# A two-block transformer on one core: another order of the conv mixer's tail

## The chip, the cores and the metric

One core of a Trainium2 chip (trn2) runs the whole program in one launch. The metric is the device time of one execution in microseconds (us); less is better. TensorE (PE) does the matrix products, VectorE (DVE), ScalarE (ACT) and GpSimd (POOL) the elementwise work, and SyncE (SP) only issues the loads.

## The reference

Two transformer blocks, one after the other, on 256 tokens of width 2048. The change lies in the first block's mixer, a gated causal convolution of width 31 per channel with a LayerNorm:

```python
mod = silu(c) @ mod_w + mod_b                # 6 vectors: shift, scale, gate, for each half of the block
h = rms_norm(x, norm1_g) * (1 + sc1) + sh1
a, gt = split(h @ conv_w_in + conv_b_in)     # 2048 -> 2 x 2048
u = a * sigmoid(gt)
u = depthwise_conv(u, conv_dw_w, 31 taps) + conv_dw_b
u = silu(layer_norm(u, conv_ln_g, conv_ln_b))
x = x + (1 + g1) * (u @ conv_w_out + conv_b_out)
# then h2 = rms_norm(x) modulated by sh2, sc2, an MLP, and a second block (attention and FFN)
```

All data are fp32. `mod_w` alone is 2048 x 12288, and it is read in 192 pieces of 128 x 1024.

## The kernel before

**Engines.** The program is written by one thread of Python that calls `A.put`, `V.put`, `T.put`, `P.put` (ACT, DVE, PE, POOL) and `Y.load` (SP). Each engine executes its own calls strictly in the order in which they were put; waits between engines are semaphores given as `after`. So where a call stands in the order of the Python code decides what stands behind it on its engine.

**Stream.** All weights come as 512 KB items through a ring of stage slots: 12 slots in the conv-in phase, 6 (`NSTAGE`) after it. The list `seq` fixes the order of items. An item is a product tile (256 rows of weights by 512 columns) or one of 16 tiles of a modulation chunk. `consume()` takes the next item and then starts what loads fit. `mix(main, extra)` spreads the extras evenly between the main items.

**Modulation.** The chunks for `0,2` (the gate) and `0,1,*` (shift and scale of the second norm) are done "aside": ACT multiplies a tile by the column of silu(c) into one of three product buffers (`R<-stage,CS`), and POOL adds it to the sum (`R<-R`); the first tile of a chunk goes straight into the sum without an add. There are 80 such tiles: `N_MOD_IN` of them are mixed into the last 46 tiles of conv-in, `N_MOD_TAIL` into the tail, and the rest into the conv-out tiles up to `N_MOD_OUT`. The last chunk (`0,1,3`, 16 tiles) is done by PE (`bank<-stage,CS`) in the tail between conv-in and conv-out.

**Conv-in.** 8 chunks p = 0..7 of 8 tiles each; chunk p gives channel tiles 2p and 2p+1 (`ct`). The first three are interleaved. `products()` calls `pe_tile(g)` and then `between_tiles()` for each tile. At the end of a chunk the task `first` copies the banks out on ACT (`scr<-bank`, "evacuation"). `gated` comes one tile later (`later(1, gated)`): 8 transposes on PE, the sigmoid on ACT, and two DVE operations that write u (`R2f<-bank,PA,scr`).

**Taps.** As soon as the u of a job in `DVE_JOBS` are there, `dve_job` puts its steps into `dve_taps`: a step is two DVE operations of 128x256 (`bank<-R2f,DW,bank`), one for each of two chains. Jobs of two channel tiles have 31 steps, the single ones, (13,) and (15,), 16 steps; then comes `end`, which copies the result out on ACT (`R2f<-bank`). ct 3 and 14 (`PE_JOBS`) are done by PE as 31 products with diagonal matrices (`bank<-R2f,hx`), in pieces of 8 taps from `pe_taps`.

**LayerNorm.** When the taps of ct 0 to 12 are over, `ln_provisional` runs one tile later: 13 PE products (26 records in the trace) sum them, DVE makes a provisional mean m0, and `slow` gets seven `centre` tasks (DVE subtracts m0 from two channel tiles), each followed by a square on ACT and its sum on PE. `ln_late(ct)` does the same for 13, 14, 15 (DVE subtraction, PE sum, ACT square, PE sum) and is called at once when the taps of such a ct end. `layer_norm()` turns the sums into mean and variance on DVE and ACT, and its `finish` tasks apply scale, Silu and the split into the two parts `hhi`, `hlo` for conv-out. Conv-out tiles are split too: ACT makes `whi`, DVE `wlo`, and PE needs three products for each fp32 product.

**What is called between two tiles** (`between_tiles`), in this order: up to two tasks, up to two delayed tasks that are due, one or more of `slow`, up to `TAPS_A_TILE` = 5 steps of `dve_taps`, one piece of `pe_taps`.

**After the last conv-in tile** the tail's two loops run (lines from `while tasks or delayed` to `layer_norm()` below). Their order of calls is what the change rewrites.

Of the kernel before, what the change touches and what calls it, by code (L numbers as in the profile page):

```python
# [11 lines left out]
ACT = mybir.ActivationFunctionType  # L12
# [4 lines left out]
NKT = D // 128  # L17
TAPS = 31
# [8 lines left out]
L_LHS = 1  # L27
L_PROJ = 6
N_MOD_IN = 66
N_MOD_TAIL = 4  # L30
N_MOD_OUT = 14
TAPS_A_TILE = 5
L_PE_JOB = 2
L_SQUARE = 2
L_SUMS = 3
# [2 lines left out]
PE_JOBS = (3, 14)  # L38
LN_LATE = (13, 14, 15)
# [69 lines left out]
def build_program(nc, a, out):  # L109
    ctx = ExitStack()  # L110
    with ctx:
        def sb(name, shape, dt=F32):
            return ctx.enter_context(nc.sbuf_tensor(name, shape, dt))

        def sem(name):
            return ctx.enter_context(nc.semaphore(name))
# [25 lines left out]
        ST = sb("ST", [128, 64])  # L142
# [12 lines left out]
        A = Engine(nc.scalar, sem("s_act"))  # L155
# [4 lines left out]
        def line(name):  # L160
# [20 lines left out]
        consts = P.put(nc.gpsimd.affine_select, out=ident[:, :], in_=ident[:, :], compare_op=ALU.not_equal,  # L181
                       fill=1.0, base=0, pattern=[[-1, 128]], channel_multiplier=1, after=[t])
        eps = ST[:, 60:61]
# [52 lines left out]
        buf, _, loaded = raw["Z"]  # L236
# [7 lines left out]
        tasks, slow = deque(), deque()  # L244
        dve_taps, pe_taps = deque(), deque()
# [4 lines left out]

        delayed, tile_no = [], [0]

        def later(n, task):

            delayed.append((tile_no[0] + n, task))
# [7 lines left out]
        def between_tiles():  # L263
            tile_no[0] += 1
            for _ in range(min(2, len(tasks))):
                tasks.popleft()()
            due = [d for d in delayed if d[0] <= tile_no[0]][:2]
            for d in due:
                delayed.remove(d)
            for d in due:  # L270
                d[1]()
            for _ in range(min(len(slow), 1 + len(slow) // 10)):
                slow.popleft()()
            for _ in range(min(len(dve_taps), TAPS_A_TILE)):
                dve_taps.popleft()()
            if pe_taps:
                pe_taps.popleft()()
# [16 lines left out]
        pair_ready = []  # L294
# [445 lines left out]
        ln = {}  # L740
# [53 lines left out]
        def diag_of(ct, j):  # L794
            return diag_store[ct][:, j // 2, 128 * (j % 2):128 * (j % 2) + 128]
# [6 lines left out]
        def pe_job(ct):  # L802

            job = {}

            def part(lo, hi_):
                if lo == 0:
                    job["bank"] = misc.take()
                b, bank, free = job["bank"]
                for j in range(lo, hi_):  # L810
                    t = T.put(nc.tensor.matmul, bank[:, 0:S], diag_of(ct, j), U[:, ct, j:j + S], start=(j == 0),
                              stop=(j == TAPS - 1), after=[diags[ct, j], u_ready[ct]] + free)
                if hi_ == TAPS:
                    conv_done[ct] = A.put(nc.scalar.activation, CV[:, ct, :], bank[:, 0:S], ACT.Identity,
                                          bias=PA[:, 48 + ct:49 + ct], after=[t, params["A"]])
                    misc.give(b, conv_done[ct])
                    conv_finished(ct)
            for lo in range(0, TAPS, 8):
                pe_taps.append(lambda lo=lo: part(lo, min(lo + 8, TAPS)))

        waiting_jobs = deque(DVE_JOBS)

# [7 lines left out]
        def conv_finished(ct):  # L830
            taps_over.add(ct)
            early = [k for k in range(NKT) if k not in LN_LATE]
            if ct in early and all(k in taps_over for k in early):
                later(1, lambda: ln_provisional(early))
            if ct in LN_LATE and "m0" in ln:
                ln_late(ct)
# [8 lines left out]
        def conv_in_epilogue(p):  # L845
            def start(pair, done, free_group):
                def first():
                    got = evacuate(pair, done)
                    free_group(got[0][2], got[1][2])

                    def gated():
                        two = [misc.take(), misc.take()]
                        for gate in (1, 0):
                            _, bank, free = two[gate]
                            for k in range(2):
                                for tok in range(2):
                                    kk = 2 * gate + k
                                    _, buf, made = got[tok]
                                    t = T.put(nc.tensor.transpose,
                                              bank[:, k * 256 + tok * 128:k * 256 + tok * 128 + 128],  # L860
                                              buf[:, kk * 128:(kk + 1) * 128], ident[:, :],
                                              after=[made, consts] + free)
                            if gate:
                                gates_in = t
                        for i, _, _ in got:
                            tiles.give(i, t)
                        i, sig, free = tiles.take()
                        for k in range(2):
                            ct = 2 * p + k
                            r = A.put(nc.scalar.activation, sig[:, k * S:(k + 1) * S], two[1][1][:, k * S:(k + 1) * S],  # L870
                                      ACT.Sigmoid, bias=PA[:, 32 + ct:33 + ct], after=[gates_in, params["A"]] + free)
                        for k in range(2):
                            ct = 2 * p + k
                            u_ready[ct] = V.put(nc.vector.scalar_tensor_tensor, out=U[:, ct, PAD:PAD + S],
                                                in0=two[0][1][:, k * S:(k + 1) * S], scalar=PA[:, 16 + ct:17 + ct],
                                                in1=sig[:, k * S:(k + 1) * S], op0=ALU.add, op1=ALU.mult,
                                                after=[t, r, params["A"], consts])
                        misc.give(two[1][0], r)
                        misc.give(two[0][0], u_ready[ct])
                        tiles.give(i, u_ready[ct])  # L880
                        jobs_ready()
                        for ct in (2 * p, 2 * p + 1):
                            if ct == PE_JOBS[1]:
                                pe_job(ct)
                            elif ct in PE_JOBS:
                                later(L_PE_JOB, lambda ct=ct: pe_job(ct))
                    later(1, gated)
                tasks.append(first)
            return start

# [60 lines left out]
        def layer_norm():  # L951
# [3 lines left out]
                          after=[ln["total"]])  # L955
            t = V.put(nc.vector.tensor_tensor, va[:, 0:S], mu[:, S:2 * S], mu[:, S:2 * S], ALU.mult,
                      after=[shift] + free)
# [2 lines left out]
            misc.give(ln["sums"][0], shift)  # L960
            misc.give(ln["squares"][0], t)
            t = A.put(nc.scalar.activation, va[:, S:2 * S], va[:, 0:S], ACT.Sqrt, bias=eps, scale=1.0, after=[t])
            shifts = mu[:, None, S:2 * S].to_broadcast([128, 2, S])
            factors = va[:, None, 0:S].to_broadcast([128, 2, S])
            pairs = range(0, NKT, 2)
# [101 lines left out]
        for q in range(4):  # L1067
            co += chunk(a["conv_w_out"][0], q * 512, 0, NKT, (hhi, hlo), s_ready,
                        residual_epilogue(q, 0, 2))
        tail = mix(mod_pairs(0, 1, 3, aside="PE", soon=True), mods[N_MOD_IN:N_MOD_IN + N_MOD_TAIL])  # L1070
        seq += tail + co[:3] + mix(co[3:N_MOD_OUT], mods[N_MOD_IN + N_MOD_TAIL:]) + co[N_MOD_OUT:]
        n_tail = n_first[0] + len(tail)
# [414 lines left out]
        products_of.freed[2] = list(params.values()) + [cond]  # L1487
        products(0, n1)
        conv_in_read[0] = pe_done[-1]
        while tasks or delayed:  # L1490
            run_one()
            for _ in range(min(len(dve_taps), 4)):
                dve_taps.popleft()()
        while dve_taps or pe_taps or slow or tasks or delayed or len(ln["late"]) < len(LN_LATE):
            for _ in range(2):
                if tasks or delayed:
                    run_one()
            if pe_taps:
                pe_taps.popleft()()
            for _ in range(min(len(dve_taps), 4)):  # L1500
                dve_taps.popleft()()
            if slow:
                slow.popleft()()
            if consumed[0] < n_tail:
                consume()
        while consumed[0] < n_tail:
            consume()
        while len(pair_ready) < 2:
            consume()
        A.put(nc.scalar.activation, ST[:, 61:62], eps, ACT.Sqrt, after=[consts])  # L1510
        layer_norm()
        ln["taps_done"] = conv_done[NKT - 1]
        products(n1, n2)
        norm_phase(1, h2_ready, pe_done[-1])
# [19 lines left out]
                       after=[pe_done[-1]])  # L1534
# [68 lines left out]
```

How the kernel before makes its waits and increments, by code:

```python
    def run(self):  # L82
        for fn, args, kw, sem, k in self.queue:
            made = fn(*args, **kw)
            if sem is not None:
                made.then_inc(sem, k)
```

## Time and profile before

| | before |
|---|---|
| median of three runs | 2721.91 us (2720.96 to 2722.74) |
| the profiled execution | 2721.52 us, span 2719.7 us |
| TensorE busy | 2549.7 us, 94% of the span |
| VectorE, ScalarE, GpSimd busy | 1693.2, 1146.8 and 618.9 us |
| mean granted clock of TensorE | 0.975 of full speed |
| last conv-in product ends, first conv-out product starts | about 331 and 423.9 us |

The profiled execution took 1.8 us more than its span and lies 0.4 us below the median. PE's busy time is modelled (a product that waits in the pipeline counts as busy), so the stages are read by starts and by what each engine waited for. Times in the rows are us from the span's start.

### The profile page before, as it was taken

To read this page: it belongs to the slowest core of one execution; us is meant where nothing else is said; L and a number is where in the kernel's file an instruction comes from. 1 tells how busy PE (TensorE), PEld (TensorE's weight loads), DVE (VectorE), ACT (ScalarE), POOL (GpSimd) and SP (SyncE) were. 2 spreads that over 40 slices of the span, in tenths; PEclk is the share of its full clock that TensorE was granted. 3 is DMA by queue.
4 is the path that set the end of the run, shared out by engine and by line. 5 is a ranking of instruction groups with operands and counts; after the bars stand their busy time and mean duration, and the time that the engine had idled before them with its cause. 6 is when DMAs were issued, how large, how long until landed. Compare 5 with 4: busy or idle time off the path is not lost. (4 is left out here: it accounts for less than half of the span.)

```text
span 2719.7 us, 29378 instructions
## 1 busy us (share of the span) xinstructions
PE 2549.7 (94%) x10784; PEld 1979.6 (73%) x10784; DVE 1693.2 (62%) x2024; ACT 1146.8 (42%) x1441; POOL 618.9 (23%) x277
## 2 busy tenths in 40 slices
PE   4899987899999999999889999989899999999998
PEld 2354445678888888887677788767688888888886
DVE  6678847667877767768563242396476655555455
ACT  2144416444343443444444454533444434443443
POOL 1058814012222222222223334434200000000000
PEclk9999988999999999999889999999899999999999
DMA  9989746668888988988644546797578766666664
GB/s 319 375 287 365 240 152 207 198 221 288 305 300 284 314 295 289 311 293 302 151 129 134 178 141 193 226 316 242 182 245 280 249 192 188 192 186 192 194 188 140
DMA packets 340158, 644.66 MB, mean 237 GB/s; under 512 B 30000, under 2 KB 63440, under 8 KB 338992
## 3 DMA queue, kind: packets, MB, share of 16 engines
q1 hardware_dynamic: 338752, 642.09, 71.9%
q8 instruction: 87, 1.43, 0.2%
q0 software_dynamic: 448, 0.43, 0.1%
q14 instruction: 55, 0.45, 0.0%
q10 hardware_dynamic: 816, 0.26, 0.0%
HBM read 640.60 MB, written 2.10 MB: 236 GB/s over the span
## 5 line engine op out<-in xcount | busy, mean ns | idle before, releaser
L84 ACT ACTIVATE whi<-stage 128x1024 fp32r<-128x1024 f32 x752 | 795.6, 1059 | 1034.2 <-PE bank L84 891.2
L84 DVE TENSOR_TENSOR wlo<-stage,whi 128x1024 fp32r<-128x1024 f32 x588 | 749.1, 1275 | 751.7 <-ACT whi L84 726.5
L84 PE MATMUL bank<-whi,hhi 128*128 128x512 f32 x2016 | 808.2, 401 | 41.7 <-DVE hlo L84 18.9
L84 PE MATMUL bank<-whi,hlo 128*128 128x512 f32 x2016 | 792.2, 393 | 0.0
L84 PE MATMUL bank<-wlo,hhi 128*128 128x512 f32 x2016 | 791.8, 393 | 0.0
L84 POOL TENSOR_TENSOR wlo<-stage,whi 128x1024 fp32r<-128x1024 f32 x164 | 411.3, 2508 | 1058.4 <-ACT whi L84 995.0
L84 PEld LDWEIGHTS bank<-whi,hhi 128*128 128x128 f32 x2016 | 383.5, 190 | 133.2 <-ACT scr L84 23.6
L84 PEld LDWEIGHTS bank<-wlo,hhi 128*128 128x128 f32 x2016 | 383.7, 190 | 80.6 <-issue 3.1
L84 PEld LDWEIGHTS bank<-whi,hlo 128*128 128x128 f32 x2016 | 382.7, 190 | 81.8
L84 PE MATMUL bank<-whi,uhi 128*128 128x512 f32 x992 | 390.0, 393 | 0.0
L84 PE MATMUL bank<-whi,ulo 128*128 128x512 f32 x992 | 389.3, 392 | 0.0
L84 PE MATMUL bank<-wlo,uhi 128*128 128x512 f32 x992 | 387.4, 391 | 0.0
L84 DVE SCALAR_TENSOR_TENSOR acc<-stage,CS,acc 128x1024 f32<-128x1024 f32 x165 | 235.5, 1427 | 18.0 <-DMA stage<-in_mod_w 14.6
L84 POOL TENSOR_TENSOR R<-R 128x1024 f32<-128x1024 f32 x75 | 183.2, 2445 | 270.4 <-ACT R L84 262.6
L84 PE MATMUL bank<-stage,hx 128*128 128x512 f32 x512 | 232.7, 613 | 10.8 <-DMA stage<-in_conv_w_in 6.6
L84 PEld LDWEIGHTS bank<-wlo,uhi 128*128 128x128 f32 x992 | 186.3, 188 | 41.4 <-issue 0.2
L84 PEld LDWEIGHTS bank<-whi,ulo 128*128 128x128 f32 x992 | 186.3, 188 | 40.8
L84 PEld LDWEIGHTS bank<-whi,uhi 128*128 128x128 f32 x992 | 186.4, 188 | 40.3 <-issue 1.1
L84 PEld LDWEIGHTS bank<-stage,hx 128*128 128x128 f32 x512 | 99.3, 197 | 134.4 <-issue 121.2
L84 DVE SCALAR_TENSOR_TENSOR bank<-R2f,DW,bank 128x256 f32<-128x256 f32 x418 | 165.4, 483 | 0.0
L84 DVE SCALAR_TENSOR_TENSOR R<-stage,CS,R 128x1024 f32<-128x1024 f32 x105 | 134.3, 1279 | 11.4 <-DMA stage<-in_mod_w 9.0
L84 PE MATMUL bank<-ident,scr 128*128 128x128 f32 x524 | 83.2, 302 | 47.0 <-DVE scr L84 41.8
(120 smaller groups left out, 1219.8 us busy)
## 6 DMA issues: line engine op xcount, KB each, us to landing
stage<-in_mlp_w SPq DMA_DIRECT2D x256, 512.0 KB, 5.4
stage<-in_mod_w SPq DMA_DIRECT2D x192, 512.0 KB, 7.1
stage<-in_w_ada SPq DMA_DIRECT2D x192, 512.0 KB, 5.4
stage<-in_w_in SPq DMA_DIRECT2D x136, 512.0 KB, 3.9
stage<-in_w_ffn_gate SPq DMA_DIRECT2D x88, 512.0 KB, 4.4
stage<-in_w_ffn_up SPq DMA_DIRECT2D x88, 512.0 KB, 4.5
stage<-in_w_ffn_down SPq DMA_DIRECT2D x88, 512.0 KB, 4.2
stage<-in_conv_w_in SPq DMA_DIRECT2D x128, 256.0 KB, 7.3
```

The source lines that it names most:

```text
L84: made = fn(*args, **kw)
```

## The change

Five edits of order, none of the arithmetic.

1. **Pace of the taps.** Instead of 5 steps a tile, `between_tiles` keeps an estimate: every tile adds 4.1 us, every step 0.8 us, and steps are put until they are 5.0 us ahead of the tiles. With no taps waiting the taps' clock is set to the tiles'.
2. **Gated units of the last chunk** (p = 7) run at once after its evacuation instead of among the delayed tasks.
3. **PE's taps** of ct 14 are one piece of 31 instead of four pieces of 8; those of ct 3 stay as they were.
4. **The tail's loop.** The first loop runs only `tasks`, and without DVE steps. In the second, PE's taps come first, then up to 3 DVE steps (4 before), then up to two tasks, one of `slow`, one item of the stream. `layer_norm()` is put right after that loop, ahead of the items that are left; before, it came behind them and behind two conv-out items. One more small ACT operation (a Silu on 128x1) is put behind LayerNorm's square root.
5. **Modulation tiles**: 9 instead of 4 in the tail, so 5 instead of 10 among the conv-out tiles (from tile 3 up to 10 instead of up to 14).

```diff
-N_MOD_TAIL = 4
-N_MOD_OUT = 14
-TAPS_A_TILE = 5
+N_MOD_TAIL = 9
+N_MOD_OUT = 10
+LEAD = 5.0
+TILE_US = 4.1
+STEP_US = 0.8
...
-            for _ in range(min(len(dve_taps), TAPS_A_TILE)):
+            pace["tile"] += TILE_US
+            if not dve_taps:
+                pace["taps"] = max(pace["taps"], pace["tile"])
+            while dve_taps and pace["taps"] < pace["tile"] + LEAD:
+                pace["taps"] += STEP_US
                 dve_taps.popleft()()
...
-            for lo in range(0, TAPS, 8):
-                pe_taps.append(lambda lo=lo: part(lo, min(lo + 8, TAPS)))
+            for lo in range(0, TAPS, 8 if ct == PE_JOBS[0] else TAPS):
+                pe_taps.append(lambda lo=lo: part(lo, min(lo + (8 if ct == PE_JOBS[0] else TAPS), TAPS)))
...
-                    later(1, gated)
+                    if p == NKT // 2 - 1:
+                        tasks.append(gated)
+                    else:
+                        later(1, gated)
...
             t = A.put(nc.scalar.activation, va[:, S:2 * S], va[:, 0:S], ACT.Sqrt, bias=eps, scale=1.0, after=[t])
+            A.put(nc.scalar.activation, ST[:, 62:63], eps, ACT.Silu, after=[consts])
...
-        while tasks or delayed:
+        while tasks:
             run_one()
-            for _ in range(min(len(dve_taps), 4)):
+        while dve_taps or pe_taps or slow or tasks or delayed or len(ln["late"]) < len(LN_LATE):
+            if pe_taps:
+                pe_taps.popleft()()
+            for _ in range(min(len(dve_taps), 3)):
                 dve_taps.popleft()()
-        while dve_taps or pe_taps or slow or tasks or delayed or len(ln["late"]) < len(LN_LATE):
             for _ in range(2):
                 if tasks or delayed:
                     run_one()
-            if pe_taps:
-                pe_taps.popleft()()
-            for _ in range(min(len(dve_taps), 4)):
-                dve_taps.popleft()()
             if slow:
                 slow.popleft()()
             if consumed[0] < n_tail:
                 consume()
+        A.put(nc.scalar.activation, ST[:, 61:62], eps, ACT.Sqrt, after=[consts])
+        layer_norm()
         while consumed[0] < n_tail:
             consume()
-        while len(pair_ready) < 2:
-            consume()
-        A.put(nc.scalar.activation, ST[:, 61:62], eps, ACT.Sqrt, after=[consts])
-        layer_norm()
```

## Rows read from the trace of the kernel before

**Rows 1.** By stage: start:end, length; busy us of PE, PEld, DVE, ACT, POOL; clock, DMA share, GB/s.

```profile
150.00:331.00 181.00, 176.83 (x493) 88.15 (x492) 154.53 (x389) 82.50 (x100) 144.28 (x67) 0.99 0.87 306
331.00:424.00 93.00, 66.54 (x215) 35.07 (x213) 47.57 (x99) 30.03 (x43) 24.01 (x11) 0.85 0.48 161
424.00:536.00 112.00, 99.33 (x416) 79.05 (x416) 79.84 (x78) 61.85 (x82) 29.78 (x10) 0.94 0.63 195
```

**Rows 2.** What ACT waited for, 210 to 331 us: us in total, times, longest.

```profile
ACT R L84 <- POOL R L84: 33.7, 23, 8.8
ACT R2f L84 <- DVE bank L84: 29.7, 4, 11.3
```

**Rows 3.** DVE in order of time, conv-in: start, us, operation, count [idle before it].

```profile
213.35 2.43 DVE L84 SCALAR_TENSOR_TENSOR bank<-R2f,DW,bank 128x256 f32<-128x256 f32 x6
216.51 0.99 DVE L84 TENSOR_SCALAR bank<-R2f,DW,PA 128x256 f32<-128x256 f32 x2 [0.73 <-ACT R2f L84]
...
243.56 0.88 DVE L84 SCALAR_TENSOR_TENSOR R2f<-bank,PA,scr 128x256 f32<-128x256 f32 x2 [2.56 <-PE bank L84]
...
256.21 1.29 DVE L84 SCALAR_TENSOR_TENSOR G<-bank,G 128x512 f32<-128x512 f32 x2
...
275.65 0.88 DVE L84 SCALAR_TENSOR_TENSOR R2f<-bank,PA,scr 128x256 f32<-128x256 f32 x2 [5.61 <-ACT scr L84]
...
307.73 0.88 DVE L84 SCALAR_TENSOR_TENSOR R2f<-bank,PA,scr 128x256 f32<-128x256 f32 x2 [5.61 <-ACT scr L84]
```

**Rows 4.** ACT in order of time around the ends of two tap jobs.

```profile
270.07 0.66 ACT L84 ACTIVATE R2f<-bank 128x256 f32<-128x256 f32 x2 [11.31 <-DVE bank L84]
270.62 1.15 ACT L84 ACTIVATE R<-stage,CS 128x1024 f32<-128x1024 f32 x1
271.66 1.09 ACT L84 ACTIVATE scr<-bank 128x512 f32<-128x512 f32 x2
...
282.55 1.15 ACT L84 ACTIVATE R<-stage,CS 128x1024 f32<-128x1024 f32 x1 [1.35 <-POOL R L84]
...
302.16 0.66 ACT L84 ACTIVATE R2f<-bank 128x256 f32<-128x256 f32 x2 [10.94 <-DVE bank L84]
```

**Rows 5.** PE in order of time, end of conv-in to the first conv-out product.

```profile
306.74 24.20 PE L84 MATMUL bank<-stage,hx 128*128 128x512 f32 x56
...
330.77 5.78 PE L84 MATMUL bank<-R2f,ones 128*128 128x256 f32 x26
344.05 3.58 PE L84 MATMUL bank<-ones,R 128*128 128x1 f32 x16 [7.50 <-POOL R L84]
348.24 1.94 PE L84 MATMUL bank<-ident,scr 128*128 128x128 f32 x8 [0.61 <-DVE MC L84]
...
358.01 5.39 PE L84 MATMUL bank<-R2f,hx 128*128 128x256 f32 x16
...
405.05 7.03 PE L84 MATMUL bank<-stage,CS 128*1 128x512 f32 x16 [1.04 <-DMA stage<-in_mod_w]
423.88 0.77 PE L84 MATMUL bank<-whi,hhi 128*128 128x512 f32 x1 [11.80 <-DVE hlo L84]
```

**Rows 6.** DVE in order of time, tail.

```profile
332.92 0.55 DVE L84 TENSOR_SCALAR bank<-R2f,DW,PA 128x256 f32<-128x256 f32 x1
...
337.05 2.26 DVE L84 TENSOR_TENSOR R2f<-R2f,scr 128x512 f32<-128x512 f32 x1
...
351.14 0.87 DVE L84 SCALAR_TENSOR_TENSOR R2f<-bank,PA,scr 128x256 f32<-128x256 f32 x2
...
361.54 0.69 DVE L84 TENSOR_TENSOR R2f<-R2f,scr 128x512 f32<-128x512 f32 x1
```

**Rows 7.** Groups of instructions, 331 to 424 us: busy us, mean ns | idle before.

```profile
L84 PE MATMUL bank<-stage,CS 128*1 128x512 f32 x64 | 28.4, 592 | 1.0 <-DMA stage<-in_mod_w 1.0
```

**Rows 8.** The same groups, 424 to 484 us, and 484 to 531 us behind the dots.

```profile
L84 DVE TENSOR_TENSOR wlo<-stage,whi 128x1024 fp32r<-128x1024 f32 x14 | 33.8, 2455 | 6.6 <-ACT whi L84 4.3 <-issue 2.3
...
L84 DVE TENSOR_TENSOR wlo<-stage,whi 128x1024 fp32r<-128x1024 f32 x17 | 20.8, 1225 | 19.7 <-ACT whi L84 19.7
```

More of the change, by code:

```diff
@@ L251, in build_program @@
         delayed, tile_no = [], [0]
+        pace = {"tile": 0.0, "taps": 0.0}
         def later(n, task):
```

## The prediction, made before the changed kernel was run

> **What bounds the kernel now.** I read the stages first, then what ACT waited for, then DVE, ACT and PE in order of time. By stage [rows 1], conv-in (150 to 331 us) keeps PE near full in the modelled figures, with the loads at 0.87 of their share. The tail (331 to 424 us) is the weak place: PE busy 66.5 of 93 us, clock 0.85, loads at 0.48. In the conv-out stage PE is busy 99.3 of 112 us. The tail is where the change works, but conv-in is where two of its edits act first, so both have to be followed.
>
> In conv-in the reader should look at ACT. It waited 29.7 us on four occasions for DVE's taps [rows 2]: it stands at the copy-out of a job that DVE has not finished, with an evacuation and modulation copies queued behind it. DVE is then idle 5.61 us before each new u, in two rounds alike [rows 3]. That is a loop: taps end, copy-out, copies, evacuation, transposes, sigmoid, u, next taps. It gives 32.1 us a round (275.65 to 307.73), where 8 tiles cost PE 27.7 (24.20 us for 7 tiles [rows 5], 3.46 each). So conv-in runs by this loop as much as by PE. The copies also wait 33.7 us for POOL [rows 2], and in such a stretch one comes every 2.5 us (1.15 and 1.35 idle [rows 4]).
>
> In the tail the chain is: last conv-in product 330.8, transposes of the last gated unit only at 348.24, behind a 7.50 us wait for POOL's last sum (344.05) [rows 5]; u at 351.14 [rows 6]; taps of 14 and 15 side by side; the modulation products; then 11.80 us of waiting for LayerNorm, conv-out from 423.88 [rows 5].
>
> **The change part by part.** All is counted as a shift of the first conv-out product, for behind it no order changes but the number of aside tiles.
>
> *Pace of the taps.* The estimate has 4.1 us a tile, PE needs 3.46. A round begins with at most one tile between empty taps and new ones, so 12 steps are put in its first tile and 5.1 a tile then; a job of 31 steps and its `end` are over 5 tiles after their start, where 5 a tile took 7. DVE works no faster for it, as it has its steps in either case; only the place of `end` in ACT's order moves, by two tiles. With 66 copies on 46 tiles (1.43 a tile) that puts some three more copies between `end` and the evacuation. The first three cost 1.04 each (three product buffers are free by then), each further one waits for POOL, 2.5 us.
> - Jobs (0,1), (2,4): these sit on a backlog in which nobody waits for the evacuation; 0. The last three steps of (2,4) no longer stand behind u of p = 3: today they run at 213.35 and (5,6) starts at 216.51 [rows 3]. Gain 3.1.
> - u of p = 4: `end` came behind the evacuation, now three copies and the evacuation come behind `end`. Taps over at 237.9, +0.6 copy-out, +3.1 copies, +1.1 evacuation, +2.3 for the next copy, transposes and sigmoid: 245.0 against 243.56. +1.4, the gain of 3.1 used up.
> - u of p = 5: between copy-out and evacuation one copy today (270.07, 270.62, 271.66 [rows 4]), then four, and two more before the sigmoid. Taps end to u goes from 5.6 to 0.6 + 3.1 + 1.4 + 1.1 + 4.9 = 11.1. +5.5.
> - u of p = 6: five copies for two, one of them a first tile of a chunk that needs no POOL, and one before the sigmoid: 9.7 for 5.6, +4.1; but DVE's two gate sums (1.29 [rows 3]) now come behind the taps, -1.3. Together +2.8.
>
> u of p = 6 comes 9.7 us later. From below: 0, if DVE's idle time takes the copies in. From above: all three rounds lose POOL two tiles of work, 3 x 2 x 1.43 x 2.45 = 21.
>
> *The provisional mean.* `end` of (11,12) is put after tile 61, so `ln_provisional` stands on PE ahead of tiles 63 and 64 instead of behind them. It needs the copy-out, 25.9 us after u of p = 6 (307.73 to 332.92 [rows 3, 6], +0.7); PE gets there after 5 tiles, 16.2 us after u. PE waits 9.7 us with two tiles of the last chunk behind it. The 26 records cost 5.8 [rows 5], and after such a wait 3 more: the first ones after idle take 5.39 for 16 (0.337 each), not 0.222 [rows 5]. Then m0, 0.4.
>
> *Gated unit first.* On PE it no longer stands behind the 7.50 us wait. But on DVE all 16 steps of job (13,) are put by tile 64, ahead of it (12.5 at 0.79 a step, 24.4 us for 31 [rows 3, 6]), with m0 and three `centre` in between. A `centre` takes 0.69 alone and 2.26 beside POOL [rows 6]; I take 2.0, POOL having a backlog. So u of p = 7 comes 25.9 + 8.8 + 0.4 + 12.5 + 6.0 = 53.6 us after u of p = 6, against 43.4 today. +10.2. With the full clock and 0.69: 46.7, +3.3. PE and ACT are ready some 8 us before DVE, which hides what they do.
>
> On the second price, the Trainium skill ("SBUF — State Buffer", section "SBUF: two separate sides") has the port pair of DVE and POOL as an exclusive lock for a whole instruction. By it each `centre` could wait for a whole POOL add, 0.69 + 2.35 = 3.0, and this step would be 3 us more; the trace's 2.26 is the one case here and stays below that.
>
> *One piece of taps.* `part` ends with `ln_late(14)`: its DVE subtraction waits for PE's 31 products and stands ahead of all taps of 15. Today they run side by side. From u of p = 7: 1.0 + 14.1 (62 records of 0.227) + 3 slow clock + 0.5 copy = 18.6; late work of 14 and 13's end 2.5; 16 steps 12.5; four `centre` 2.8; mod columns 1.4; end of 15 and its late work 2.5: 40.3. Today about 38.
>
> *LayerNorm first, five more tiles.* Six passes of the loop take only three PE tiles; 14 stand behind the last square. At 0.444 a record, four a tile [rows 7], 24.9 us. The loads are slower: 19 items are outstanding when the slots move again (19 tail and conv-out items; a full share would be 306/0.87 = 352 GB/s, 1.49 us an item [rows 1]; I take 1.42, a little better than that mean, with nothing else on the queue), 27.0 + 1.8 for the first slot + 1.2 landing = 30. LayerNorm itself and its waits lie under that. Left at the end: one `whi`, two Silu, `hhi`, `hlo`, 3.4. So conv-out starts 40.3 + 33.4 = 73.7 after u of p = 7, today 72.7 (351.14 to 423.88). +1.0. The 11.80 us wait [rows 5] shrinks to some 8, and the five tiles (7.1 us of loads) take the rest. From below -6 (loads well ahead), from above +6. The small Silu costs 0.2 and moves a table load under the tiles.
>
> *Conv-out.* Beside POOL's adds `wlo` takes 2455 ns, without them 1225 [rows 8]; 15 tiles last 60 us there, the next 17 only 47. Of the 18.6 us over, slow clock, LayerNorm's finish and the mod columns have some 8; the ten aside tiles about 1.0 each. Five fewer: -5, bounds -2 and -9.
>
> **Sum:** 9.7 + 10.2 + 1.0 - 5.0 = +15.9, on the profiled 2721.5 us: 2737.4; the median lies 0.4 above that run. I say 2737.5.
>
> **Rivals.**
> - *The gated unit wins its 12 us.* The 7.50 us wait and the 4.2 us of mod columns behind it (344.05 to 348.24 [rows 5]) are no longer ahead of it: u 11.7 earlier, -11.7 + 1 - 5 = -15.7, 2706. For it: the 7.50 us wait is real. It decides if less than half of job (13,) stands ahead of that unit on DVE and `end` costs ACT nothing. Against it: 332.92 plus m0, three `centre` and 12.5 is past 347 even if no one waits. Chance 0.10.
> - *Nothing in sum.* The earlier `end` is taken in by idle time (0), the provisional wait costs its lower bound (+3.3), +1, -5: 2721. For it: PE ran 56 records without a gap in the last round, and only POOL and DVE sums are behind the copies. Chance 0.18.
> - *POOL bounds conv-in.* It is busy 144 of 181 us [rows 1]; if every stop of ACT is lost to it, the first term is 21: 2749, and up to 2752 with 3 us of port waits. Chance 0.10.
> - The forecast, 2729 to 2746: 0.60. The rest, 0.02, is beyond.
>
> **Range and chances.** 0.2% is 5.4 us, about what a measurement of this kernel tells from no change. 2714 to 2752 leaves out the first rival and what lies above the third. Slower: the forecast, the third rival and a part of the second, 0.73; within 0.2%: 0.14; faster: 0.13. Most of the chance is on one side; the likeliest case's own range is 2729 to 2746.
>
> **What would show it.** Right: ACT idle before `R2f<-bank` grows from about 11 to 15 us and more in the rounds of p = 5 and 6, and DVE's idle time before u from 5.61 to about 11 and 10; PE idle about 10 us before `bank<-R2f,ones`, with 16 conv-in records behind it; u of p = 7 near 371; DVE idle some 15 us until PE's taps of 14 are over; conv-out near 444. Wrong: u of p = 6 by 309; the sums ahead of all conv-in products on PE without a wait; u of p = 7 before 350; conv-out before 424. Most fragile is the count of copies behind `end`: if stage items are late there, ACT waits for DMA and not for POOL, and the first term changes.

## The result, and the profile after

The changed kernel took 2736.21 us (median of five runs, 2729.96 to 2737.79) against 2721.91 (five runs, 2720.07 to 2723.47): a ratio of 1.0047, 95% interval 1.0032 to 1.0062. It is 14.3 us slower. The profiled execution took 2732.52 us, span 2730.7.

One thing has to be known before the two traces are compared: the programs do not start alike. The first u is written at 153.29 us in the kernel before and at 150.35 in the changed one; over the fourteen traces of this study (one of each kernel) it lies between 150.35 and 155.37, and what follows it in conv-in repeats to 0.1 us wherever the order is the same. So places are given below from the first u. The last conv-out stage ends with the first transposes of the next norm (536.44 before, 545.95 after).

| us from the first u | before | after | shift | forecast shift |
|---|---|---|---|---|
| u of p = 3 | 59.3 | 61.2 | +1.9 | 0 |
| u of p = 6 | 154.4 | 165.8 | +11.3 | +9.7 |
| u of p = 7 | 197.9 | 210.7 | +12.8 | +19.9 |
| first conv-out product | 270.6 | 287.8 | +17.2 | +20.9 |
| first transposes behind conv-out | 383.2 | 395.6 | +12.4 | +15.9 |

The places put the loss at 12.4 us. The medians differ by 14.3, and the spans of the two profiled executions by 11.0: the changed one had its first u 2.9 us earlier and lost 1.5 behind the last place of the table.

The last conv-in round and the loop through ACT, in order of time. First DVE, with the first two u (before, the second came 8.74 us behind the first) and the rounds that answer to [rows 3]. Three dots mark lines left out:

```profile
150.35 0.88 DVE L86 SCALAR_TENSOR_TENSOR R2f<-bank,PA,scr 128x256 f32<-128x256 f32 x2 [13.46 <-PE bank L86]
...
152.03 12.63 DVE L86 SCALAR_TENSOR_TENSOR bank<-R2f,DW,bank 128x256 f32<-128x256 f32 x32
164.56 0.88 DVE L86 SCALAR_TENSOR_TENSOR R2f<-bank,PA,scr 128x256 f32<-128x256 f32 x2
...
243.41 0.88 DVE L86 SCALAR_TENSOR_TENSOR R2f<-bank,PA,scr 128x256 f32<-128x256 f32 x2 [6.64 <-ACT scr L86]
...
281.10 0.88 DVE L86 SCALAR_TENSOR_TENSOR R2f<-bank,PA,scr 128x256 f32<-128x256 f32 x2 [11.21 <-ACT scr L86]
...
306.28 1.28 DVE L86 SCALAR_TENSOR_TENSOR G<-bank,G 128x512 f32<-128x512 f32 x2
316.13 0.88 DVE L86 SCALAR_TENSOR_TENSOR R2f<-bank,PA,scr 128x256 f32<-128x256 f32 x2 [8.56 <-ACT scr L86]
```

The idle times 2.56, 5.61 and 5.61 [rows 3] have become 6.64, 11.21 and 8.56 (with the gate sums, now behind the taps, 9.8 from taps to u). What fills them is on ACT, to be read against [rows 4]: the copy-out waits 15.41 us instead of 11.31, and behind it stand four modulation copies, not one, before the evacuation (`scr<-bank`).

```profile
269.92 0.66 ACT L86 ACTIVATE R2f<-bank 128x256 f32<-128x256 f32 x2 [15.41 <-DVE bank L86]
270.46 3.22 ACT L86 ACTIVATE R<-stage,CS 128x1024 f32<-128x1024 f32 x3
274.13 1.15 ACT L86 ACTIVATE R<-stage,CS 128x1024 f32<-128x1024 f32 x1 [0.45 <-POOL R L86]
275.19 1.06 ACT L86 ACTIVATE scr<-bank 128x512 f32<-128x512 f32 x2
```

Over 210 to 331 us ACT's wait for the taps is 43.0 us, against 29.7 [rows 2] (us in total, times, longest):

```profile
ACT R2f L86 <- DVE bank L86: 43.0, 3, 15.4
ACT R L86 <- POOL R L86: 28.8, 22, 8.8
```

PE from the provisional mean to conv-out, against [rows 5]:

```profile
333.69 4.91 PE L86 MATMUL bank<-R2f,ones 128*128 128x256 f32 x22
341.88 2.08 PE L86 MATMUL bank<-R2f,ones 128*128 128x256 f32 x4 [3.28 <-ACT R2f L86]
343.75 7.65 PE L86 MATMUL bank<-stage,hx 128*128 128x512 f32 x16
...
361.95 15.37 PE L86 MATMUL bank<-R2f,hx 128*128 128x256 f32 x62 [7.34 <-DVE R2f L86]
...
427.83 1.88 PE L86 MATMUL bank<-stage,CS 128*1 128x512 f32 x4 [0.47 <-DMA stage<-in_mod_w]
438.17 0.77 PE L86 MATMUL bank<-whi,hhi 128*128 128x512 f32 x1 [8.46 <-ACT scr L86]
```

The sums do stand ahead of 16 conv-in records, but 22 of their 26 records run without waiting; only the last four, for the channels just copied out, wait, and that for 3.28 us. Behind that wait the granted clock is 0.50 (341.8 to 343.7 us), and the four records take 2.08 us where the 22 took 4.91. And DVE, against [rows 6]: three `centre` of 2.57, 1.37 and 0.68 us, then u of p = 7, then 15.97 us of nothing until PE's taps of 14 are over.

```profile
344.45 2.57 DVE L86 TENSOR_TENSOR R2f<-R2f,scr 128x512 f32<-128x512 f32 x1
...
350.92 1.37 DVE L86 TENSOR_TENSOR R2f<-R2f,scr 128x512 f32<-128x512 f32 x1
...
356.91 0.68 DVE L86 TENSOR_TENSOR R2f<-R2f,scr 128x512 f32<-128x512 f32 x1
...
361.04 0.86 DVE L86 SCALAR_TENSOR_TENSOR R2f<-bank,PA,scr 128x256 f32<-128x256 f32 x2
377.87 0.42 DVE L86 TENSOR_TENSOR R2f<-R2f,scr 128x256 f32<-128x256 f32 x1 [15.97 <-ACT R2f L86]
```

The end of the chain, from the last modulation tile (over at 429.71) to the first conv-out product (438.17), on ACT and then on DVE:

```profile
430.51 1.06 ACT L86 ACTIVATE whi<-stage 128x1024 fp32r<-128x1024 f32 x1 [0.21 <-DMA stage<-in_conv_w_out]
431.87 1.06 ACT L86 ACTIVATE whi<-stage 128x1024 fp32r<-128x1024 f32 x1 [0.30 <-DMA stage<-in_conv_w_out]
433.23 1.06 ACT L86 ACTIVATE whi<-stage 128x1024 fp32r<-128x1024 f32 x1 [0.30 <-DMA stage<-in_conv_w_out]
434.19 1.08 ACT L86 ACTIVATE scr<-R2f,PA 128x256 f32<-128x256 f32 x2
435.30 0.63 ACT L86 ACTIVATE hhi<-scr 128x512 fp32r<-128x512 f32 x1
...
436.01 1.41 DVE L86 TENSOR_TENSOR R2f<-R2f,scr 128x512 f32<-128x512 f32 x2
437.33 0.69 DVE L86 TENSOR_TENSOR hlo<-scr,hhi 128x512 fp32r<-128x512 f32 x1
```

### The profile page after: what moved, and what is told of

Read it like the earlier page. It is cut to its first block and busy times, and to the rows that moved or that the text cites. A ratio compares the mean times of both kernels' runs of the same rounds, so it can differ in the third digit from the quotient of the medians.

```text
span 2730.7 us, 29383 instructions
## 1 busy us (share of the span) xinstructions
PE 2550.4 (93%) x10784; PEld 1976.8 (72%) x10784; DVE 1685.0 (62%) x2024; ACT 1146.9 (42%) x1442; POOL 613.6 (22%) x277
## 5 line engine op out<-in xcount | busy, mean ns | idle before, releaser
L86 DVE TENSOR_TENSOR wlo<-stage,whi 128x1024 fp32r<-128x1024 f32 x588 | 738.6, 1257 | 758.3 <-ACT whi L86 735.3
L86 PEld LDWEIGHTS bank<-whi,hhi 128*128 128x128 f32 x2016 | 384.0, 190 | 125.2 <-ACT scr L86 22.2
L86 POOL TENSOR_TENSOR R<-R 128x1024 f32<-128x1024 f32 x75 | 177.7, 2370 | 270.7 <-ACT R L86 263.3
```

The source lines that it names most:

```text
L86: made = fn(*args, **kw)
```

## The experiments

Twelve kernels, four to a chip. Ratios are to the kernel before on the same chip; its median was 2723.49, 2722.52 and 2722.19 us on the three chips. The steps are compared by their places in us from the first u, in this table; "u6" and "u7" are the u of p = 6 and 7, and "LN" is the DVE operation that forms the variance.

| | ratio (95%) | u6 | u7 | LN | conv-out | behind conv-out |
|---|---|---|---|---|---|---|
| before | 1 | 154.4 | 197.9 | 263.8 | 270.6 | 383.2 |
| after | 1.0047 (1.0032 to 1.0062) | 165.8 | 210.7 | 251.4 | 287.8 | 395.6 |
| e1 old pace | 0.999 (0.9978 to 1.0003) | 154.4 | 189.8 | 238.0 | 274.1 | 382.0 |
| e2 new pace alone | 1.0084 (1.0071 to 1.0097) | 165.8 | 220.1 | 284.8 | 291.6 | 404.1 |
| e3 DVE's taps first | 1.0014 (1.0006 to 1.0023) | 165.8 | 208.3 | 239.6 | 278.0 | 384.0 |
| e4 LayerNorm behind | 1.0057 (1.0044 to 1.0069) | 165.8 | 210.7 | 251.3 | 290.5 | 397.2 |
| e5 tiles as before | 1.004 (1.0025 to 1.0056) | 165.8 | 210.7 | 252.5 | 282.5 | 393.3 |
| e6 gated unit later | 1.0055 (1.004 to 1.007) | 165.8 | 221.8 | 257.2 | 295.0 | 402.6 |
| e8 mean later | 1.0058 (1.0043 to 1.0073) | 165.8 | 205.2 | 254.1 | 291.6 | 399.5 |
| e9 = e1 + e3 | 0.998 (0.9971 to 0.9989) | 154.4 | 189.9 | 231.3 | 268.4 | 375.5 |
| e11 = e3, pace 3.46, lead 0 | 0.9996 (0.9986 to 1.0005) | 151.7 | 183.2 | 242.0 | 273.0 | 381.0 |
| e12 = e9 + items ahead | 0.9944 (0.9929 to 0.9959) | 154.4 | 189.8 | 236.8 | 262.5 | 369.4 |
| e13 = e9 + finish ahead | 0.996 (0.9944 to 0.9975) | 154.4 | 189.8 | 231.4 | 266.7 | 373.1 |
| e14 = e12 + e13 | 0.9945 (0.9928 to 0.9962) | 154.4 | 189.8 | 238.7 | 262.6 | 369.8 |

**e1: the pace undone.**

```diff
-            while dve_taps and pace["taps"] < pace["tile"] + LEAD:
-                pace["taps"] += STEP_US
+            for _ in range(min(len(dve_taps), 5)):
                 dve_taps.popleft()()
```

> The changed kernel with 5 steps a tile again. My theory: the pace puts the copy-out of each tap job two tiles earlier in ACT's order, and costs 8.4 us by the u of p = 6 and keeps all 16 steps of job (13,) ahead of the last gated unit. So u of p = 6 returns to about 307.7, the sums of the provisional mean start without a wait, u of p = 7 comes at about 344, conv-out starts at about 419, and the time is about 2716. Rival (the pace is harmless, the tail's other edits cost the time): u of p = 6 stays near 316 and the time near 2736.

Measured: 2720.44 us, 0.999. u of p = 6 is back at 154.4, to the tenth, and u of p = 7 comes at 189.8, 8.1 before the old place. The rival is out. But conv-out comes at 274.1, not some 5 earlier: the 16 us in which DVE waits for PE's taps now have eight steps of 13 and all 16 of 15 behind them. In the changed kernel the pace thus costs 13.7 us at the first conv-out product. The other four edits together are worth 1.2 us at the end of conv-out, and nothing that the runs can tell from no change.

**e2: the pace alone**, in the kernel before, with the changed kernel's estimate.

> The kernel before with the new pace of the taps and nothing else. My theory: DVE's idle time before u grows from 2.6, 5.6 and 5.6 us to about 6.6, 11 and 8.6 in the three rounds, u of p = 6 comes at about 317, u of p = 7 at about 361, and the time is about 2732. Rival (the pace only costs together with the other edits): within 3 us of the kernel before, 2722.

Measured: 1.0084, 21 us at the end of conv-out. More than I expected. U of p = 6 is 11.4 late, for the 9 expected, and u of p = 7 is 22.2 late, not 10. PE shows why:

```profile
367.33 1.22 PE L86 MATMUL bank<-R2f,ones 128*128 128x256 f32 x2 [7.98 <-DVE R2f L86]
...
373.13 1.97 PE L86 MATMUL bank<-ident,scr 128*128 128x128 f32 x8 [0.52 <-DVE MC L86]
```

The 8 records at 373.13 are the last gated unit. With the new pace job (13,) ends before it in the order, so the late work of 13 stands ahead of it on PE (7.98 us of waiting), and the mod columns too. In the changed kernel the gated unit is put first.

**e6: the last gated unit among the delayed tasks again**, in the changed kernel.

```diff
-                    if p == NKT // 2 - 1:
-                        tasks.append(gated)
-                    else:
-                        later(1, gated)
+                    later(1, gated)
```

> The changed kernel with the last gated unit among the delayed tasks again. My theory: with the new pace the late work of 13 and the mod columns come ahead of it on PE, and u of p = 7 comes some 9 us later, as it did with the pace alone; conv-out some 8 us later; time about 2744. Rival (DVE's 16 steps of 13 stand ahead of that u in either order, so the order on PE is hidden, as my prediction had it): at most 2 us, 2738.

u of p = 7 comes 11.1 us later and conv-out 7.2 later, as the theory says; the rival (hidden by DVE) is out. The timed ratio, 1.0055, is only 0.0008 above that of the changed kernel and the intervals overlap; the place of the steps is shown, the size at the end (2 us by the ratios, 7 by the places) stays open. Beside e2 it says what the edit does under the new pace: it takes back what the pace would otherwise cost there.

**e8: the provisional mean behind all conv-in products.**

```diff
-                later(1, lambda: ln_provisional(early))
+                later(3, lambda: ln_provisional(early))
```

> The changed kernel with the provisional mean put two tiles later, behind all conv-in products, where it stood before. Theory A (what the trace of the changed kernel shows): only the last two of 13 products waited, 3.3 us, and DVE 2.6; so u of p = 7 comes some 3 us earlier and conv-out 1 to 3 us; time about 2733. Theory B (my prediction's price for that step): 10 us at u of p = 7, time about 2726.

u of p = 7 comes 5.5 us earlier: more than theory A's 3, far from B's 10. But conv-out comes 3.8 later. Two of the three `centre` tasks that stood ahead of u now come among the taps of 15, and the last squares end later. DVE waits for their sums (5.16), and in the drain PE waits 3.28 us for one load:

```profile
407.78 0.42 DVE L86 SCALAR_TENSOR_TENSOR scr<-bank,scr 128x256 f32<-128x256 f32 x1 [5.16 <-PE bank L86]
```

Both theories missed that. So these tasks delay u where they stand in the changed kernel, and still cost conv-out less there than behind it. That the two waits are the reason is read from the trace; no run tests it.

**e3: DVE's taps before the late work of 14**, PE's piece left whole.

```diff
                 if hi_ == TAPS:
+                    while ct == PE_JOBS[1] and dve_taps:
+                        dve_taps.popleft()()
                     conv_done[ct] = A.put(...
```

> The changed kernel, PE's taps of 14 still one piece, but all of DVE's taps of 13 and 15 are put before the copy-out and late work of 14. My theory: DVE's wait of 16 us for PE's taps goes, 15 ends with 14, the last late square comes some 16 us earlier, conv-out starts at about 425 instead of 438, and the time is about 2723. Rival (the tail is bound by its loads and the modulation products, so that the late work lies beside them anyway): conv-out moves by under 4 us, 2733 or more.

Measured: 1.0014, which is 9 us less than the changed kernel by the ratios, and conv-out 9.8 earlier, where some 13 were expected. DVE has no such wait any more; the steps of 15 run beside PE's:

```profile
365.78 11.45 DVE L86 SCALAR_TENSOR_TENSOR bank<-R2f,DW,bank 128x256 f32<-128x256 f32 x29
377.68 0.42 DVE L86 TENSOR_TENSOR R2f<-R2f,bank 128x256 f32<-128x256 f32 x1 [0.45 <-ACT R2f L86]
...
380.18 0.42 DVE L86 TENSOR_TENSOR R2f<-R2f,scr 128x256 f32<-128x256 f32 x1 [1.62 <-ACT R2f L86]
```

The variance is formed 11.8 us earlier, 2 us of which are lost to the leftover items behind them. The rival (under 4 us) is out.

**e4: LayerNorm behind the leftover modulation.** `layer_norm()` and the table load ahead of it moved behind the loop that drains the tail.

> The changed kernel with LayerNorm put behind the leftover modulation again (but ahead of the conv-out items). My theory: LayerNorm's arithmetic, 5 us on DVE and ACT with a table load, comes behind the last tile; PE's wait of 8.46 us before conv-out grows to about 12, and the time to about 2740. Rival (the wait is set by the loads and splits of the conv-out items, not by LayerNorm): no change, 2736.

Conv-out comes 2.7 later; PE's wait before it is 10.65 instead of 8.46; ratio 1.0057. The direction is as expected, the size smaller. So LayerNorm's place makes some 2 us of the old wait of 11.80 us [rows 5].

**e5: 4 and 14 for the modulation tiles again.**

> The changed kernel with 4 modulation tiles in the tail and 10 among the conv-out tiles again. My theory: they cost the same in either place, about 7 us as loads in the tail and about 5 us beside POOL in conv-out, so conv-out starts some 7 us earlier and lasts some 5 us longer; time about 2734. Rival (the move is what the change lives by): 2741 or more.

Conv-out starts 5.3 us earlier and lasts 3.0 longer; ratio 1.004. By the places the five tiles cost 2.3 us more in the tail than among the conv-out tiles; the intervals of the ratios overlap. The rival (2741 or more) is out.

**e9: e1 and e3 together.**

> The changed kernel with 5 steps a tile again and DVE's taps of 13 and 15 put before the copy-out and late work of 14. My theory: the two edits' savings add up until the loads bind: the last late square comes at about 380 us, conv-out starts at about 421, and the time is about 2714, faster than the kernel before. Rival (behind the late work the tail is bound by loads that start too late, so that the second edit is worth nothing beside the first): 2720.

Measured: 2717.18 us, 0.998: faster than both kernels, but 5 us, not 8. Against the kernel before, the variance is formed 32.5 us earlier (part of it because LayerNorm no longer stands behind the leftover items), but conv-out starts only 2.2 us earlier: five more modulation tiles now lie in between, and in the drain PE waits for loads.

```profile
383.93 8.74 PE L86 MATMUL bank<-stage,CS 128*1 128x512 f32 x20
395.71 10.23 PE L86 MATMUL bank<-stage,CS 128*1 128x512 f32 x20 [3.03 <-DMA stage<-in_mod_w]
```

**e11: the estimate's numbers from the trace.** e3 with `LEAD = 0.0` and `TILE_US = 3.46`.

> The kernel of e3 (DVE's taps put before the late work of 14) with the estimate's numbers set from the trace: 3.46 us a tile instead of 4.1, and no lead. My theory: the loss in conv-in comes from the numbers, which put the copy-out before DVE can have finished; with these a job's end comes at the eighth tile and behind the evacuation. u of p = 6 then comes at or before its place in the kernel before (154.4 us after the first u, against 165.8), and the time is about 2716. Rival (any estimate of this kind costs it, through the burst of steps at a job's start): 162 us or more, about 2725.

u of p = 6 comes at 151.7, 2.7 us *before* its old place and 14 before the changed kernel's; the rival (162 or more) is out. Ahead of that u DVE waits 0.24 us, for 8.56 in the changed kernel. It was the numbers, not the idea; which of the two numbers did it was not told apart. Ahead of the u of p = 5 DVE still waits 6.70 us. The time gained less than expected (2720.85 for 2716, 0.9996): the job (11,12) now ends in the tail, so the provisional mean waits for it, 8.85 us on PE:

```profile
362.14 8.57 PE L86 MATMUL bank<-R2f,ones 128*128 128x256 f32 x26 [8.85 <-ACT R2f L86]
```

**e12: seven stream items ahead of PE's taps**, on e9.

```diff
         while tasks:
             run_one()
+        for _ in range(7):
+            consume()
```

> The kernel of e9 with seven stream items (four modulation tiles for PE, three copies for ACT) put right behind the last gated unit, ahead of PE's taps. My theory: since the stage slots stand full for some 50 us before PE takes the first modulation tile, the drain behind LayerNorm is bound by loads that start late; PE waits 4.5 us for u there anyway. Conv-out starts some 8 us earlier than in e9 (268.4 us after the first u), at about 260; time about 2709. Rival (the copies for ACT wait for POOL's backlog and hold up 13's copy-out behind them): no gain or a loss, 2717 or more.

Measured: 2706.93 us, 0.9944. Four modulation tiles lie where PE waited for u. The slot of a tile done aside comes free when ACT's copy has read it, and SyncE's longest wait for such a copy between 320 and 400 us is 18.2 us here, against 44.6 in e9 (34.2 in the kernel before, 48.3 in the changed one). The loads resume 188.3 us behind the first u, 26 us earlier than in e9. PE still waits 5.90 us for one of them, and the variance is formed 5.5 us later than in e9, but conv-out comes at 262.5, 6 us before e9. So the loads set the start of conv-out there, and not the variance. By the ratios e12 is 10 us faster than e9, which ran on another chip; the places give 6.

```profile
343.89 5.28 PE L86 MATMUL bank<-stage,CS 128*1 128x512 f32 x8 [5.90 <-DMA stage<-in_mod_w]
349.96 3.59 PE L86 MATMUL bank<-stage,CS 128*1 128x512 f32 x8 [0.79 <-DMA stage<-in_mod_w]
353.48 13.65 PE L86 MATMUL bank<-R2f,hx 128*128 128x256 f32 x62
```

**e13: two finish tasks ahead of the leftover modulation**, on e9.

```diff
         layer_norm()
+        for _ in range(2):
+            tasks.popleft()()
```

> The kernel of e9 with LayerNorm's first two finish tasks put ahead of the leftover modulation. My theory: PE's wait of 8.4 us before conv-out is three whi in a row, then Silu, hhi, two DVE subtractions and products, hlo; with the first two pairs done before, only whi and wlo are left, and conv-out starts some 4 to 5 us earlier, at about 264 us after the first u; time about 2713. Rival (the landing of the third conv-out item sets the start): under 1 us.

PE's last wait halves as expected, 4.26 us, now for `wlo`. Conv-out comes 1.7 us before e9, not 4 to 5: earlier on PE waited 5.27 us for a load, against 3.03 in e9. The ratio is 0.996 (2710.56 us).

```profile
400.27 10.76 PE L86 MATMUL bank<-stage,CS 128*1 128x512 f32 x20 [5.27 <-DMA stage<-in_mod_w]
...
421.78 0.76 PE L86 MATMUL bank<-whi,hhi 128*128 128x512 f32 x1 [4.26 <-DVE wlo L86]
```

**e14: both.**

> The kernel of e9 with both edits of e12 and e13. My theory: they act on different parts of the tail, the loads and the last chain of operations, and add up: conv-out at about 255 us after the first u, time about 2704. Rival (they save the same wait): no better than the better of the two.

2708.04 us, 0.9945: no better than e12. The rival holds. The first product starts after 3.30 instead of 8.44 us, but it does so at the same place, because a wait for a load of 4.71 us comes before it:

```profile
406.19 7.37 PE L86 MATMUL bank<-stage,CS 128*1 128x512 f32 x12 [4.71 <-DMA stage<-in_mod_w]
416.86 0.47 PE L86 MATMUL bank<-whi,hhi 128*128 128x512 f32 x1 [3.30 <-DVE wlo L86]
```

## Why the prediction was right, and where it was not

The time was right (2737.5 for 2736.2), and so was the first mechanism. That it came out within 1.3 us was luck: one step was 8.7 us too dear, two were 1.9 and 3.4 too cheap, and by the places the whole was 3.5 too dear (12.4 for 15.9).

*Pace of the taps: right.* The three rounds were forecast at +1.4, +5.5 and +2.8; the places give +0.9, +5.6 and +2.9 (after a shift of 1.9 at u of p = 3). Taps to u: forecast 7.1, 11.1 and 9.7, measured 6.6, 11.2 and 9.8. e1 shows the cause by undoing it, e11 by changing two numbers. Missed: of job (0,1), 17 steps stand on DVE ahead of u of p = 1, not 10. That u comes 14.2 us behind the first instead of 8.7, and PE waits 1.15 us for it. I had put that backlog at 0; by u of p = 3 it is 1.9. The gain of 3.1 behind that u did come, as no taps of (2,4) are left there.

*The provisional mean: mis-sized.* "It needs the copy-out": only the last two of its 13 products do. I let all 26 records wait, and charged 3 us of slow clock for it: 25.9 + 8.8 us. Measured: 22 records run at once and the wait is 3.28. The clock does fall behind it, to 0.50, but only the last four records and the start of the next product meet it: some 1 us on the four (2.08 us, where the 22 took 0.223 each). The mean is there 27.9 us after u of p = 6 and not 35.1. The three `centre` took 4.6, not 6.0. Step forecast +10.2, measured +1.5 (44.9 against 43.4).

*Gated unit first: half right.* It is true that DVE's 16 steps of 13 bound u of p = 7 in the changed kernel (PE had the transposes done at 354.6, ACT the sigmoid at 355.1, u came at 361.0). But I compared with the old order and not with the old place under the new pace: there, the late work of 13 comes first (e2, e6), 11 us at u. With the old pace u of p = 7 does come 8 us earlier than before (e1), with eight steps of 13 ahead of it on DVE, not twelve, and the mod columns behind. The gated unit's place and the tail's new loop make that together; they were not told apart. The rival was real at u, but of its 15.7 us nothing clear is left in e1's time (0.999): conv-out comes 3.5 later than before, and e9 takes 5.7 of that order back.

*One piece of taps: right.* DVE idle "some 15 us", measured 15.97; from u to the variance 40.7 and to the last square's sum 40.1, forecast 40.3 for that sum. e3 and e9 show what the late work of 14 ahead of DVE's taps costs: 10 us at conv-out with the new pace, and 5.7 with the old.

*LayerNorm and five more tiles: too cheap by 3.4.* From u of p = 7 to conv-out 77.1 us, forecast 73.7. The loads were not the cause: PE's last modulation tiles do wait for them one by one (1.01, 0.74, 0.47 and the like), but end 28.6 us after the last square's sum, for a forecast of 30 (of which the 1.8 and 1.2 for the first slot and the landing stood without a row). The mis-sized term is what is left at the end: 3.4 forecast, 8.46 measured. The sum had one `whi` there. Three stand there, each started when its load had landed, and the third ends at 434.29; and the first `hlo` stands on DVE behind two LayerNorm operations of the next pair (1.41). The text of the prediction itself said "some 8" for that wait, which its sum did not use. In e1, e3, e9, e11 and e12 it is 8.39 to 8.48 as well.

*Conv-out: right in size, not in parts.* -5 forecast, all of it for the five tiles; -4.8 measured, of which e5 finds 3.0 to be the five tiles. The other 1.8 stay open.

The three `centre` ahead of u took 2.57, 1.37 and 0.68 us, and the longest such operation in any trace took 2.84 (e11). So the prediction's 3.0 was not passed, and as a price for each of the three it would have been too much. It also called 2.26 the one case at hand; the kernel before has a second beside a POOL add, of 1.63 us. The Trainium skill ("SBUF — State Buffer", "SBUF: two separate sides") says that a DVE operation with two SBUF inputs and a POOL operation that reads SBUF take their shared port pair as an exclusive lock, for the whole instruction. The traces agree with that as a bound.

## What to carry to other kernels

An instruction that waits and is put early in program order is not done early, it is a barrier on its engine. When a pace or a look-ahead moves work, follow the operation that waits for its end (here a copy-out on ACT) and count what is queued behind it, with the limit of that work (here POOL, up to 2.5 us a copy) and not only its length. Set the numbers of an estimate from the trace's own stage: with 4.1 us a tile and 5.0 of lead, u of p = 6 came 11 us late; with 3.46 and 0 it came 2.7 early. An edit that takes part of such a loss back looks like a gain (the gated unit first, e6). And before tuning the last chain of a stage, see whether the loads ran while the engines waited: seven items put earlier brought conv-out 6 us forward, where the five edits together put it 17 us back.

## What the runs showed that I had not expected

- The start of a program varies by 5 us (first u at 150.35 to 155.37 us), and behind it conv-in repeats to 0.1 us: 154.4 for u of p = 6 in six profiles, 165.8 in seven. A difference of a few us is safer read from such places than from medians over a few runs.
- A DVE subtraction of 128x512 in SBUF takes 0.69 us, and up to 2.57 beside POOL's adds in the changed kernel (2.84 in e11). The taps, which read one large operand from SBUF and one from a bank, take 469 to 498 ns an operation in all fourteen traces, beside POOL's adds or not.
- PE's wait before conv-out went from 8.44 to 3.30 us (e12 to e14) and the start of conv-out did not move.
